# Weighted sums of the first heads moved ahead of a query tile, and four of sixteen picks of seven heads summed on another engine

## The chip, the cores and the metric

One core of a Trainium2 chip runs the whole program. The metric is the device time of one execution in microseconds (us). The engines are TensorE (PE), VectorE (DVE), ScalarE (ACT), GpSimd (POOL) and SyncE (SP), and 16 DMA engines move data.

## What is computed

Two transformer blocks on 512 tokens of width 1024. All that the change touches is the last stage of the second one, a mixture of 16384 experts with one row each, of which every token takes 16 in each of 8 heads. Shortened:

```python
def peer_ffn(x, w_q, k1, k2, down, up):
    # per block of 128 tokens
    q = x @ w_q                                  # 8 heads x 256
    s1, s2 = q1 @ k1, q2 @ k2                    # 128 scores each
    t1, t2 = top16(s1), top16(s2)
    w, idx = top16(all pairs t1 + t2)            # 16 of 256
    g = softmax(w)
    h = gelu(x . down[idx])                      # one dot per pick
    return sum(g * h * up[idx])                  # over 8 heads x 16 picks
```

The result is added to the residual, normalised and stored.

## The kernel before

The tokens lie in 4 tiles of 128, one token on each partition. A *head* in the code is one of 32 pairs of a token tile and a head of the expert stage (`N_HEADS`); head i belongs to tile i // 8. Each head has 16 *picks*, so there are 512, numbered n = 16 i + s. For a pick, an indirect DMA, issued by POOL in the function `gather`, fetches one row of `peer_rows` for each of the 128 tokens: 8 KB, `down` in its first half and `up` in its second, 1 MB in all. It lands in one of the buffers of `pair`. There are 7 of these at first; 6 more come in at picks 75, 76, 83, 107, 108 and 120 (`MORE_PAIRS`).

What happens to pick s of head i, in order:

- `dot(i, s)` on DVE (line 2534) multiplies the `down` half by the tokens and sums it over the row.
- `expert_weights(i, b)` on ACT takes the GELU of two such sums, b = s // 2; `weights(i, b)` on DVE (line 2541) multiplies them by the softmax; ACT then writes two diagonal matrices with the weights on the diagonal (`diag`, 12 buffers). `head_weights(i, first, stop)` is a run of such pairs. Within it, ahead of pair 5, stands `softmax_exp(i + 2)`.
- `weighted(i, first, stop)` on PE (line 1120) multiplies each diagonal by the `up` half in two matmuls and adds the product up in PSUM. Its end (`up_used`) is what the next gather into that buffer waits for.

DVE also runs the search of the top 16 for a later head, in steps between the dots (`best_keys` to `expert_numbers`, lines 2427 to 2499). In head 0 (`first_head`) these are the steps of heads 1 and 2.

At the same time the query projection is still being computed for all heads: 16 tiles, `query(t)` on PE, 24 matmuls each, and `peer_scores(h)` behind each pair. The weights of a tile come by a DMA of SP into a ring of few slots, and are split into two parts: ACT writes the high part (`query_high`, called high(t) here), and POOL subtracts it for the low part (`query_low`, low(t) here, line 2699). The load of tile t from 6 on waits for the end of `query(t - 2)`. POOL works its list in order: gathers 0 to 4, low(5), gathers 5 and 6, low(6), gathers 7 to 10, low(7), gathers 11 to 14, low(8), gathers 15 to 18, low(9), gathers 19 to 22, and so on to low(15). So gather 11 stands behind low(7), which stands behind high(7) on ACT.

No scheduler is at work: every engine runs its instructions in the order in which they are written, and waits on semaphores. ACT's list starts as

```python
peer_scores(1); query(4); query(5); query_high(6)
head_weights(0, 0, 2); peer_scores(2); softmax_exp(1)
head_weights(0, 2, 6); query_high(7); query(6)
head_weights(0, 6, 10); query_high(8); query(7)
head_weights(0, 10, 14); query_high(9); peer_scores(3)
```

where `query` and `peer_scores` on ACT copy PE's result out of PSUM. ACT's table of functions has to be loaded anew (`ACT_TABLE_LOAD`) between GELU and Exp.

## Time and profile before

| | |
|---|---|
| median of 3 runs | 3074.2 us (3073.37 to 3075.46) |
| the profiled execution's own time | 3077.88 us |
| its span in the profile | 3076.1 us |
| PE busy | 2693.7 us (88%) |
| DVE busy | 1747.6 us (57%) |
| POOL busy | 1157.1 us (38%) |
| ACT busy | 881.3 us (29%) |
| gathers (queue q0) | 73728 packets, 536.90 MB |

The page cuts the span into 40 slices of 77 us. The row of GB/s rises from 22 in slice 22 to 150, 339, 409, 411 and then stands at 427 to the last slice but one, while PE falls from nine tenths to seven. The stage of the gathers is the stretch from 1750 us to the end. A row of a stretch (windows) gives the busy time of each engine in it, the granted clock of PE as a share of 2.4 GHz, the busy share of the DMA engines and what they moved.

### The profile page before, as it was taken

How to read it: one execution, taken by the hardware profiler on the slowest of the kernel's cores; microseconds unless marked ns; L12 is line 12 of the kernel's file. 1: busy time of each engine (PE TensorE's matmuls, PEld its weight loads, DVE VectorE, ACT ScalarE, POOL GpSimd, SP SyncE). 2: the span in 40 equal slices, each digit the busy share in tenths (PEclk: the TensorE clock that was granted, in tenths of full speed). 3: DMA queues.
4: the chain of work that ended last, by engine and by line, in shares of the span. 5: the costliest groups of instructions: out<-in, count | busy, mean ns of one | idle time of the engine just before them, and what ended most of it. 6: DMA issues, size and time to landing. Idle time of an engine off the chain costs nothing.

```text
span 3076.1 us, 29817 instructions
## 1 busy us (share of the span) xinstructions
PE 2693.7 (88%) x10970; PEld 1857.5 (60%) x10970; DVE 1747.6 (57%) x3667; ACT 881.3 (29%) x1677; POOL 1157.1 (38%) x763
## 2 busy tenths in 40 slices
PE   6999999989989999899978899988777777777776
PEld 4999899977668888788837755543323233322222
DVE  5666762032747604322175477767777777777665
ACT  3111132134542224222142333333222222222221
POOL 1222233223934444423110355545444444444441
PEclk8999999989999999999988999999999999999999
DMA  6455431212025523212200489999999999999996
GB/s 244 158 182 176 162 127 57 62 62 76 22 69 169 173 96 94 91 62 69 71 0 22 150 339 409 411 427 427 427 427 427 427 427 427 427 427 426 427 427 288
DMA packets 125231, 722.07 MB, mean 235 GB/s; under 512 B 14864, under 2 KB 16144, under 8 KB 58288
## 3 DMA queue, kind: packets, MB, share of 16 engines
q0 software_dynamic: 73728, 536.90, 41.7%
q1 hardware_dynamic: 35920, 127.74, 12.1%
q10 hardware_dynamic: 15456, 55.80, 5.6%
q8 instruction: 72, 1.18, 0.1%
q14 instruction: 55, 0.45, 0.0%
HBM read 718.29 MB, written 2.10 MB: 234 GB/s over the span
## 4 chain that ended last, share of the span: by engine, by line
PE 58%; DMA 27%; DVE 9%; ACT 3%; issue 2%; POOL 1%; SPq 0%; ACTq 0%; DVEq 0%; POOLq 0%
PE acc L619 14%; PE acc L620 14%; PE acc L621 14%; DMA wring<-in_peer_rows,squares 9%; DMA hid<-in_peer_rows,squares 8%; PE sums L1120 5%; DMA arena<-in_peer_rows,squares 4%; DMA resid<-in_peer_rows,squares 3%; PE acc L1120 3%; PE sums L552 1%; DMA modw<-in_peer_rows,squares 1%; DVE hid L2534 1%; DVE squares L1924 1%; ACT hid L1179 1%; PE acc L843 1%
## 5 line engine op out<-in xcount | busy, mean ns | idle before, releaser
L2699 POOL TENSOR_TENSOR wring_parts<-wring,wring_parts 128x1024 fp32r<-128x1024 f32 (+1 forms) x215 | 524.2, 2449 | 1180.8 <-ACT wring_parts L1179 1180.6
L619 PE MATMUL acc<-hid_parts,wring_parts 128*128 128x384 f32 (+1 forms) x2152 | 796.2, 370 | 48.6 <-DVE hid_parts L1871 19.6
L621 PE MATMUL acc<-hid_parts,wring_parts 128*128 128x384 f32 (+1 forms) x2152 | 777.2, 361 | 0.0
L620 PE MATMUL acc<-hid_parts,wring_parts 128*128 128x384 f32 (+1 forms) x1656 | 598.6, 361 | 0.0
L619 PEld LDWEIGHTS acc<-hid_parts,wring_parts 128*128 128x128 f32 x2152 | 407.9, 190 | 116.5 <-issue 50.2
L621 PEld LDWEIGHTS acc<-hid_parts,wring_parts 128*128 128x128 f32 x2152 | 407.5, 189 | 38.5
L1179 ACT ACTIVATE wring_parts<-wring 128x1024 fp32r<-128x1024 f32 (+1 forms) x215 | 223.1, 1040 | 514.0 <-DMA wring<-in_w_ffn_out 196.7
L620 PEld LDWEIGHTS acc<-hid_parts,wring_parts 128*128 128x128 f32 x1656 | 314.9, 190 | 32.9 <-issue 5.5
L2711 POOL DMA_INDIRECT arena<-in_peer_rows,squares x180 | 200.5, 1114 | 244.8 <-PE acc L1120 153.4
L1179 ACT ACTIVATE hid<-hid 128x2 f32<-128x2 f32 (+2 forms) x293 | 67.1, 229 | 764.6 <-DVE arena L2534 237.6
L2711 POOL DMA_INDIRECT wring<-in_peer_rows,squares x158 | 176.7, 1118 | 199.3 <-PE acc L1120 144.2
L620 PE MATMUL acc<-arena_parts,wring_parts 128*128 128x384 f32 (+1 forms) x656 | 236.4, 360 | 0.0
L2711 POOL DMA_INDIRECT hid<-in_peer_rows,squares x109 | 116.1, 1065 | 152.6 <-PE acc L1120 122.5
L1946 DVE TENSOR_TENSOR arena<-squares,acc 128x384 f32<-128x384 f32 (+1 forms) x66 | 39.5, 599 | 219.7 <-ACT squares L1179 219.7
L2534 DVE SCALAR_TENSOR_TENSOR arena<-arena,resid 128x1024 f32<-128x1024 f32 x101 | 127.2, 1260 | 47.0 <-DMA arena<-in_peer_rows,squares 46.4
L2534 DVE SCALAR_TENSOR_TENSOR arena<-arena 128x1024 f32<-128x1024 f32 x79 | 96.9, 1227 | 61.1 <-DMA arena<-in_peer_rows,squares 60.8
L620 PEld LDWEIGHTS acc<-arena_parts,wring_parts 128*128 128x128 f32 x656 | 123.2, 188 | 13.4 <-issue 0.7
L1974 DVE SCALAR_TENSOR_TENSOR resid<-acc,halfg,resid 128x384 f32<-128x384 f32 (+3 forms) x32 | 16.2, 547 | 199.0 <-PE acc L621 199.0
L1179 ACT ACTIVATE squares<-acc 128x384 f32<-128x384 f32 (+1 forms) x66 | 34.8, 527 | 321.8 <-PE acc L621 269.4
L2534 DVE SCALAR_TENSOR_TENSOR wring<-wring,arena 128x1024 f32<-128x1024 f32 x78 | 95.6, 1226 | 52.7 <-DMA wring<-in_peer_rows,squares 52.3
L2534 DVE SCALAR_TENSOR_TENSOR wring<-wring,resid 128x1024 f32<-128x1024 f32 x80 | 101.0, 1263 | 42.2 <-DMA wring<-in_peer_rows,squares 41.7
L1120 PE MATMUL acc<-arena,tmp 128*128 128x512 f32 x184 | 88.6, 617 | 24.9 <-ACT tmp L1179 24.9
(422 smaller groups left out, 4284.1 us busy)
## 6 DMA issues: line engine op xcount, KB each, us to landing
wring<-in_w_ffn_in SPq DMA_DIRECT2D x88, 512.0 KB, 4.7
modw<-in_w_ada ACTq DMA_DIRECT2D x56, 512.0 KB, 3.6
modw<-in_w_mod ACTq DMA_DIRECT2D x48, 512.0 KB, 3.8
wring<-in_w_ffn_out SPq DMA_DIRECT2D x32, 512.0 KB, 3.5
wring<-in_w_in SPq DMA_DIRECT2D x28, 512.0 KB, 3.4
wring<-in_w_mix_in SPq DMA_DIRECT2D x18, 512.0 KB, 3.4
wring<-in_peer_w_q SPq DMA_DIRECT2D x16, 512.0 KB, 5.7
wring<-in_w_ffn_out SPq DMA_DIRECT2D x16, 384.0 KB, 3.1
```

The lines of the kernel that those rows point to most:

```text
L552: return nc.tensor.matmul(o, w, x, start=(k == 0), stop=(k == last))
L619: nc.tensor.matmul(o, wh, high, start=first, stop=False)
L620: nc.tensor.matmul(o, wh, low, start=False, stop=False)
L621: return nc.tensor.matmul(o, wl, high, start=False, stop=last)
L843: mm = nc.tensor.matmul(acc[:, 2 * side + hf, 0:HALF], qT[rows, both, t * P:(t + 1) * P], kdup[rows, both // 2, hf * HALF:(hf + 1) * HALF] ...
L1120: mm = nc.tensor.matmul(o[:, hf, :], diag[n % N_DIAG], pair[PAIR_OF[n]][:, D + hf * 512:D + (hf + 1) * 512], start=(at == 0), stop=(at == ...
L1179: return nc.scalar.activation(o, i, func, **kw)
L1924: ins = V.scalar_tensor_tensor(o, Mw[:, x % 2, k, :], col, o, ALU.mult, ALU.add)
L1946: free(V.tensor_tensor(arena[:, (f * sides + hf) * width:(f * sides + hf + 1) * width], sg[:, (base + u) % 2, 0:width], acc[:, 2 * ((base ...
L2534: V.scalar_tensor_tensor(rows, rows, 1.0, xb[i // PEER_H], ALU.mult, ALU.mult, accum_out=p_dot[:, s:s + 1]).then_inc(dots_done, 1)
L2699: nc.gpsimd.tensor_tensor(Wlor[:, p, 0:blocks, 0:cols], Wlo[:, p, 0:blocks, 0:cols], Whir[:, p, 0:blocks, 0:cols], ALU.subtract).then_inc( ...
L2711: nc.gpsimd.indirect_dma_start(pair[PAIR_OF[n]], None, a["peer_rows"], bass.IndirectOffsetOnAxis(ap=idx_all[:, n:n + 1], axis=0)).then_inc ...
```

## The change

First, the order on PE and ACT in head 0. The weighted sum of picks 0 and 1 now stands ahead of the sixth query tile, `query(5)`; picks 2 to 5 stand ahead of `peer_scores(2)`, picks 6 and 7 ahead of `query(6)`, picks 8 to 11 ahead of `query(7)`, 12 and 13 ahead of `peer_scores(3)`. ACT's list follows: the first pair of weights ahead of the copies of `query(4)` and `query(5)` and of high(6), `softmax_exp(1)` behind six picks instead of two, high(7) behind eight instead of six, high(8) behind twelve instead of ten.

Second, in heads 0 to 6 the picks s = 1, 5, 9 and 13 (28 in all, `BY_VECTOR`) are taken off PE. ACT writes no diagonal for them. DVE multiplies the `up` half by the weight and adds it to `vector_sum`, 1024 columns of constants no longer in use; `vector_pick(i, s)` stands right behind `dot(i, s + 1)`. The gather into the buffer of such a pick waits for DVE (`vector_used`). `finish(0)` adds `vector_sum` to the sum in PSUM. POOL's list and SP's are as before.

```diff
 FIRST_PAIRS = 7
 MORE_PAIRS = {75: 7, 76: 8, 83: 9, 107: 10, 108: 11, 120: 12}
+BY_VECTOR = [i * PEER_K + s for i in range(7) for s in (1, 5, 9, 13)]
+BY_TENSOR = [_n for _n in range(N_PICKS) if _n not in BY_VECTOR]
+
+
+def tensor_picks(n):
+
+    return n - sum(m < n for m in BY_VECTOR)
...
                 for n in range(i * PEER_K + first, i * PEER_K + stop):
-                    at = n % SLOTS
-                    pe.wait_ge(diag_ready, n + 1)
+                    if n in BY_VECTOR:
+                        continue
+                    at, d = n % SLOTS, tensor_picks(n)
+                    pe.wait_ge(diag_ready, d + 1)
...
             query(4)
+            pe.wait_ge(tile_read, 1)
+            weighted(0, 0, 2)
             query(5)
+            weighted(0, 2, 6)
             peer_scores(2)
-            pe.wait_ge(tile_read, 1)
-            weighted(0, 0, 4)
+            weighted(0, 6, 8)
             query(6)
-            weighted(0, 4, 8)
+            weighted(0, 8, 12)
             query(7)
-            weighted(0, 8, 12)
+            weighted(0, 12, 14)
             peer_scores(3)
-            weighted(0, 12, 16)
+            weighted(0, 14, 16)
...
             peer_scores(1)
+            head_weights(0, 0, 2)
             query(4)
+            query_high(6)
             query(5)
-            query_high(6)
-            head_weights(0, 0, 2)
+            head_weights(0, 2, 6)
             peer_scores(2)
             softmax_exp(1)
-            head_weights(0, 2, 6)
+            head_weights(0, 6, 8)
             query_high(7)
             query(6)
-            head_weights(0, 6, 10)
+            head_weights(0, 8, 12)
             query_high(8)
             query(7)
-            head_weights(0, 10, 14)
+            head_weights(0, 12, 14)
             query_high(9)
...
+            def vector_pick(i, s):
+
+                n = i * PEER_K + s
+                if n in BY_VECTOR:
+                    k = BY_VECTOR.index(n)
+                    up, weight = pair[PAIR_OF[n]][:, D:2 * D], p_w[:, s:s + 1]
+                    dve.wait_ge(weights_ready, i * (PEER_K // BATCH) + s // BATCH + 1)
+                    if k == 0:
+                        V.tensor_scalar(vector_sum, up, weight, None, ALU.mult).then_inc(vector_used, 1)
+                    else:
+                        dve.wait_ge(vector_used, k)
+                        V.scalar_tensor_tensor(vector_sum, up, weight, vector_sum, ALU.mult, ALU.add).then_inc(vector_used, 1)
...
-                if PAIR_FREE[n]:
-                    pool.wait_ge(up_used, PAIR_FREE[n])
+                before = PAIR_FREE[n]
+                if before is not None and before in BY_VECTOR:
+                    pool.wait_ge(vector_used, BY_VECTOR.index(before) + 1)
+                elif before is not None:
+                    pool.wait_ge(up_used, tensor_picks(before) + 1)
```

How the instructions stand on ACT from the copy of `peer_scores(1)` to the first two diagonals, before. Line 1179 is the helper that every ACTIVATE goes through; `resid<-acc` copies a query tile, `wring_parts<-wring` is a high part, `hid<-hid 128x2` the GELU of a pair, `squares`, `modrows` and `tmp<-cst,hid` are diagonals:

```order
L1179 ACTIVATE arena<-acc 128x4x256 [waits acc_ready]
L1179 ACTIVATE resid<-acc 128x512 [waits acc_ready] x2
L1179 ACTIVATE wring_parts<-wring 128x1024 [waits w_loaded0]
L1179 ACT_TABLE_LOAD
L1179 ACTIVATE hid<-hid 128x2 [waits dots_done]
L1179 ACTIVATE squares<-cst,hid 128x128 [waits weights_ready]
L1179 ACTIVATE squares<-cst,hid 128x128
```

And in the changed kernel, where the helper is line 1194:

```order
L1194 ACTIVATE arena<-acc 128x4x256 [waits acc_ready]
L1194 ACT_TABLE_LOAD
L1194 ACTIVATE hid<-hid 128x2 [waits dots_done]
L1194 ACTIVATE squares<-cst,hid 128x128 [waits weights_ready]
L1194 ACTIVATE resid<-acc 128x512 [waits acc_ready]
L1194 ACTIVATE wring_parts<-wring 128x1024 [waits w_loaded0]
L1194 ACTIVATE resid<-acc 128x512 [waits acc_ready]
```

The GELU of picks 0 and 1 and the one diagonal left of them moved ahead of both query copies and of high(6).

The second place, ACT from `peer_scores(2)` on, before. `hid<-hid 128x16` is the exponential of a softmax; the high part is high(7):

```order
L1179 ACTIVATE arena<-acc 128x4x256 [waits acc_ready]
L1179 ACT_TABLE_LOAD
L1179 ACTIVATE hid<-hid 128x16 [waits top_ready]
L1179 ACT_TABLE_LOAD
L1179 ACTIVATE hid<-hid 128x2 [waits dots_done]
L1179 ACTIVATE squares<-cst,hid 128x128 [waits weights_ready]
L1179 ACTIVATE squares<-cst,hid 128x128
L1179 ACTIVATE hid<-hid 128x2 [waits dots_done]
L1179 ACTIVATE modrows<-cst,hid 128x128 [waits weights_ready]
L1179 ACTIVATE modrows<-cst,hid 128x128
L1179 ACTIVATE wring_parts<-wring 128x1024 [waits w_loaded1]
```

And now, the weights of picks 6 and 7 being the pair between the second table load and high(7):

```order
L1194 ACTIVATE arena<-acc 128x4x256 [waits acc_ready]
L1194 ACT_TABLE_LOAD
L1194 ACTIVATE hid<-hid 128x16 [waits top_ready]
L1194 ACT_TABLE_LOAD
L1194 ACTIVATE hid<-hid 128x2 [waits dots_done]
L1194 ACTIVATE modrows<-cst,hid 128x128 [waits weights_ready]
L1194 ACTIVATE modrows<-cst,hid 128x128
L1194 ACTIVATE wring_parts<-wring 128x1024 [waits w_loaded1]
L1194 ACTIVATE resid<-acc 128x512 [waits acc_ready]
```

Picks 2 to 5 left this place for one ahead of `peer_scores(2)`; high(7) still follows the exponential, and now stands behind picks 6 and 7 as well.

## Rows read from the trace of the kernel before

**Rows 1.** The page: the span, and the queue of the gathers.

```profile
span 3076.1 us, 29817 instructions
...
q0 software_dynamic: 73728, 536.90, 41.7%
```

**Rows 2.** The chain that ended last: start, us, what.

```profile
3061.49 1.24 DVE hid L2534 x2
```

**Rows 3.** Stretches of the stage: busy (instructions) of PE, PEld, DVE, ACT, POOL; clock, DMA, GB/s.

```profile
1775.00:1800.00 25.00, 25.00 (x75) 14.35 (x74) 22.09 (x61) 8.64 (x19) 14.56 (x10) 0.92 0.80 289
1800.00:1850.00 50.00, 47.73 (x160) 27.36 (x159) 34.86 (x91) 19.66 (x42) 27.42 (x21) 1.00 0.98 379
1850.00:1900.00 50.00, 44.75 (x137) 24.64 (x136) 37.97 (x88) 14.81 (x36) 29.21 (x21) 0.98 1.00 411
1900.00:1950.00 50.00, 48.07 (x145) 25.96 (x144) 35.05 (x85) 15.94 (x37) 27.74 (x21) 0.98 1.00 410
1950.00:2000.00 50.00, 46.99 (x164) 27.47 (x163) 35.65 (x115) 14.03 (x36) 21.57 (x20) 0.97 1.00 411
...
2100.00:2300.00 200.00, 156.02 (x337) 62.28 (x336) 149.34 (x404) 59.24 (x154) 92.05 (x82) 0.97 1.01 427
```

**Rows 4.** Stretches of 5 us, the same columns.

```profile
1770.00:1775.00 5.00, 1.38 (x2) 0.84 (x3) 2.81 (x7) 4.00 (x7) 2.34 (x1) 0.70 0.52 216
1775.00:1780.00 5.00, 5.00 (x8) 1.84 (x7) 3.51 (x11) 3.56 (x7) 0.96 (x1) 0.62 0.17 26
```

**Rows 5.** POOL in order of time: start us, us, then what ended the idle time.

```profile
1777.65 0.96 POOL L2711 DMA_INDIRECT hid<-in_peer_rows,squares  x1 [4.62 <-PE sums L1120]
...
1785.31 2.40 POOL L2699 TENSOR_TENSOR wring_parts<-wring,wring_parts 128x1024 fp32r<-128x1024 f32 x1
1790.89 0.96 POOL L2711 DMA_INDIRECT arena<-in_peer_rows,squares  x1 [3.18 <-PE sums L1120]
...
1803.22 0.96 POOL L2711 DMA_INDIRECT arena<-in_peer_rows,squares  x1 [3.69 <-PE sums L1120]
...
1813.90 1.84 POOL L2711 DMA_INDIRECT wring<-in_peer_rows,squares  x1 [0.16 <-issue]
```

**Rows 6.** ACT in order of time: high(6), table load, diagonals, exponential, copy.

```profile
1769.55 1.06 ACT L1179 ACTIVATE wring_parts<-wring 128x1024 fp32r<-128x1024 f32 x1 [1.80 <-DMA wring<-in_peer_w_q]
1770.63 1.28 ACT L1179 ACT_TABLE_LOAD   x1
...
1773.08 0.69 ACT L1179 ACTIVATE squares<-cst,hid 128x128 f32<-128x128 f32 x2 [0.95 <-DVE hid L2541]
...
1777.10 0.31 ACT L1179 ACTIVATE hid<-hid 128x16 f32<-128x16 f32 x1 [1.12 <-DVE hid L2463]
...
1788.93 0.60 ACT L1179 ACTIVATE resid<-acc 128x512 f32<-128x512 f32 x1 [3.91 <-PE acc L621]
```

**Rows 7.** DMA issues by line: count, KB each, median us from issue to landing.

```profile
wring<-in_peer_w_q SPq DMA_DIRECT2D x16, 512.0 KB, 5.7
```

**Rows 8.** DVE in order of time: a step of head 1's search, two dots.

```profile
1763.45 0.41 DVE L2447 TENSOR_TENSOR hid<-hid 128x256 f32<-128x256 f32 x1
...
1827.35 1.23 DVE L2534 SCALAR_TENSOR_TENSOR hid<-hid,resid 128x1024 f32<-128x1024 f32 x1 [0.80 <-DMA hid<-in_peer_rows,squares]
...
1848.86 4.00 DVE L2534 SCALAR_TENSOR_TENSOR hid<-hid,resid 128x1024 f32<-128x1024 f32 x1 [0.52 <-DMA hid<-in_peer_rows,squares]
```

**Rows 9.** PE in order of time: `query(4)`'s first and last matmul, `peer_scores(2)`, picks.

```profile
1755.97 0.48 PE L619 MATMUL acc<-hid_parts,wring_parts 128*128 128x512 f32 x1
...
1761.29 0.39 PE L621 MATMUL acc<-hid_parts,wring_parts 128*128 128x512 f32 x1
...
1767.86 2.02 PE L1086 MATMUL acc<-modw,resid 128*128 128x128 f32 x16 [0.73 <-issue]
1773.62 3.75 PE L1120 MATMUL sums<-hid,squares 128*128 128x512 f32 x4 [3.74 <-ACT squares L1179]
...
1811.10 3.60 PE L1120 MATMUL sums<-wring,squares 128*128 128x512 f32 x8
```

More of the change, by code:

```diff
@@ L130 @@
     PAIR_OF.append(_slot)
-    PAIR_FREE.append(_last.get(_slot, -1) + 1)
+    PAIR_FREE.append(_last.get(_slot))
     PAIR_USE.append(PAIR_OF.count(_slot))
@@ L511, in build @@
         dots_done, gelu_ready, weights_ready = sem("dots_done"), sem("gelu_ready"), sem("weights_ready")
-        diag_ready, up_used = sem("diag_ready"), sem("up_used")
+        diag_ready, up_used, vector_used = sem("diag_ready"), sem("up_used"), sem("vector_used")
+        at = CONST["dup0"][0]
+        vector_sum = cst[:, at:at + D]
         ssq_ready, fstd_ready, fin_ready = sem("ssq_ready"), sem("fstd_ready"), sem("fin_ready")
@@ L1116, in weighted @@
                 for n in range(i * PEER_K + first, i * PEER_K + stop):
-                    at = n % SLOTS
-                    pe.wait_ge(diag_ready, n + 1)
+                    if n in BY_VECTOR:
+                        continue
+                    at, d = n % SLOTS, tensor_picks(n)
+                    pe.wait_ge(diag_ready, d + 1)
                     for hf in range(2):
-                        mm = nc.tensor.matmul(o[:, hf, :], diag[n % N_DIAG], pair[PAIR_OF[n]][:, D + hf * 512:D + (hf + 1) * 512],
+                        mm = nc.tensor.matmul(o[:, hf, :], diag[d % N_DIAG], pair[PAIR_OF[n]][:, D + hf * 512:D + (hf + 1) * 512],
                                               start=(at == 0), stop=(at == SLOTS - 1))
@@ L1734, in expert_weights @@
                 for n in range(first, first + BATCH):
-                    if n >= N_DIAG:
-                        act.wait_ge(up_used, n - N_DIAG + 1)
-                    run(diag[n % N_DIAG], ident, ACT.Copy, scale=p_w[:, n % PEER_K:n % PEER_K + 1]).then_inc(diag_ready, 1)
+                    if n in BY_VECTOR:
+                        continue
+                    d = tensor_picks(n)
+                    if d >= N_DIAG:
+                        act.wait_ge(up_used, d - N_DIAG + 1)
+                    run(diag[d % N_DIAG], ident, ACT.Copy, scale=p_w[:, n % PEER_K:n % PEER_K + 1]).then_inc(diag_ready, 1)
             def final_std(t):
@@ L2542, in weights @@
                                 ALU.mult).then_inc(weights_ready, 1)
+            def vector_pick(i, s):
+                n = i * PEER_K + s
+                if n in BY_VECTOR:
+                    k = BY_VECTOR.index(n)
[6 more added lines that the diff above has]
+                        V.scalar_tensor_tensor(vector_sum, up, weight, vector_sum, ALU.mult, ALU.add).then_inc(vector_used, 1)
             def finish(t):
@@ L2550, in finish @@
                     emptied(dve, UNIT["rows"] + w)
-                dve.wait_ge(up_used, (t + 1) * SLOTS)
-                V.tensor_tensor(sum_, total[:, :, :].rearrange("p a n -> p (a n)"), g2row,
-                                ALU.mult).then_inc(tile_read, 1)
+                dve.wait_ge(up_used, tensor_picks((t + 1) * SLOTS))
+                products = total[:, :, :].rearrange("p a n -> p (a n)")
+                if t == 0:
+                    dve.wait_ge(vector_used, len(BY_VECTOR))
+                    link(V.tensor_tensor(vector_sum, vector_sum, products, ALU.add))
+                    products = vector_sum
+                V.tensor_tensor(sum_, products, g2row, ALU.mult).then_inc(tile_read, 1)
                 dve.wait_ge(tile_read, CREDIT + t + 1)
@@ L2572, in head @@
                 dot(i, 2)
+                vector_pick(i, 1)
                 if more:
@@ L2586, in head @@
                 dot(i, 6)
+                vector_pick(i, 5)
                 if more:
@@ L2600, in head @@
                 dot(i, 10)
+                vector_pick(i, 9)
                 if more:
@@ L2614, in head @@
                 dot(i, 14)
+                vector_pick(i, 13)
                 if more:
@@ L2629, in first_head @@
                 dot(0, 2)
+                vector_pick(0, 1)
                 best_pairs(1)
@@ L2643, in first_head @@
                 dot(0, 6)
+                vector_pick(0, 5)
                 key_numbers(1)
@@ L2656, in first_head @@
                 dot(0, 10)
+                vector_pick(0, 9)
                 best_pairs(2)
@@ L2670, in first_head @@
                 dot(0, 14)
+                vector_pick(0, 13)
                 key_numbers(2)
```

## The prediction

> **What bounds the kernel now.** I read the page first. The span is 3076.1 us, and 536.90 MB of it go through the gathers' queue [rows 1], 512 picks of 1.049 MB. Then the chain that ended last: its final link out of the DMA is the dot at 3061.49 [rows 2], and 14.6 us of sums and normalising follow. Then the stretches [rows 3]: from 2100 on the DMA engines are full (share 1.01) at 427 GB/s, with PE at 78% and DVE at 75%. A gather costs 1.049 MB / 427 GB/s = 2.46 us there, and nothing on PE or DVE makes that shorter. So the change can only move the end by what it does to the DMA engines' idle and slow time before 2000.
>
> How much is that? Against 427 GB/s, the five stretches from 1775 to 2000 [rows 3] lack 25 x 138/427 = 8.1 us, 50 x 48/427 = 5.6, 1.9, 2.0 and 1.9: 19.5 us. One hole is plain: shares of 0.52 and 0.17 between 1770 and 1780 [rows 4] are 2.4 + 4.2 = 6.6 us idle. It begins when gathers 0 to 6 have landed; gather 7 is issued only at 1777.65, after waiting for PE [rows 5]. The DMA engines take it up some 1.6 us after the issue (share 0.17 of the 5 us up to 1780).
>
> PE is no strict bound there. It is busy 89 to 100% [rows 3], and four picks fewer per head would free about 1.75 us each (3.60 us for two picks, which overlap a little [rows 9]): 28 picks, 49 us. DVE takes 28 x 1.23 = 34 us more [rows 8]; it is busy 166 of 225 us [rows 3], 74%, and goes to some 83%. Both lie beside a full DMA, and I cost both at nothing; if DVE were late, the buffers would come free later, and that is the third rival.
>
> **Part one, the earlier first sums.** Step by step, with durations of before.
>
> - Gathers 7 to 10. DVE ends head 1's `candidates` at 1763.9 [rows 8], so weights(0, 0) is at 1764, the diagonal just behind, and pick 0 starts on PE at about 1764.6 instead of 1773.62 [rows 9]. PE had ended `query(4)` at 1761.7 [rows 9] and idled 3 us. Pick 0 takes 3.55 us at the lower clock as before (3.75 with overlap, granted 0.70 and 0.62 [rows 4, 9], mostly the 1.2 GHz level). POOL is not free, though: low(6) needs high(6), which waits for its load and runs at 1769.55 to 1770.6 [rows 6] in both orders; low(6) then takes 2.4 us [rows 5]. Gather 7 goes out at 1773.2, 4.4 us earlier. Gather 8 (a buffer that DVE frees) follows at 1775.3. `query(5)` on PE, 5.7 us [rows 9], now ends at 1773.8, its copy 0.6 later [rows 6], and only then comes the GELU of picks 2 and 3: they are used at 1777.1 and 1778.8, gathers 9 and 10 go out right behind. The first hole shrinks from 6.6 to 2.3 us (1772.6 to 1774.9).
>
> - Gather 11. Pick 4 is done at 1781.6, `peer_scores(2)` 2.0 us later [rows 9], its copy at 1784.6. Then table load 1.28, the exponential and its sum 0.5, table load 1.28 [rows 6]: 1787.7. Before, all this stood behind two picks and ahead of the GELU of picks 2 and 3. Now it delays picks 6 and 7, whose diagonals end at 1788.9, and behind them high(7), 1.06 [rows 6], and low(7), 2.4: 1792.4. Gather 11 goes out at 1792.5, against 1790.89 [rows 5], although its buffer was free at 1781.6. The four gathers 7 to 10 with one weight load of 0.524 MB (1.2 us) keep the DMA for 11.1 us, to 1786.0; it then idles until 1794.2: 8.2 us.
>
> - Gather 15. PE was idle for 5 us, so picks 6 and 7 take 3.55 + 1.8, to 1794.0, and `query(6)` ends at 1799.5; the load for tile 8 waits for it. Its copy 1800.3, GELU and weights of picks 8 and 9 at 1800.8. Then DVE has two dots, a vector pick and search steps of head 2 (3 x 1.23 [rows 8] and about 2 us, an estimate) before the second exponential can run: 1806.5. Exponential, table load, GELU, weights, two diagonals (0.7 [rows 6]): 1809.5; high(8), low(8): 1813.1. Gather 15 goes out at 1813.2 against 1803.22 [rows 5]: 10 us late. DMA idle from 1805.3 to 1814.9: 9.6 us.
>
> - Gather 19. Picks 10 and 11 restart PE again, 1809.3 to 1814.6; `query(7)` to 1820.0; the load for tile 9 is issued only then and takes some 5.7 us [rows 7]; high(9) and low(9) to 1829.0. Gather 19 goes out at 1829.2 against 1813.90 [rows 5]: 15 us late. DMA idle 1826.0 to 1830.9: 4.9 us.
>
> So the holes are 2.3 + 8.2 + 9.6 + 4.9 = 25 us by gather 19. To see the net I compare landings: the dot of pick 21 waited for its DMA and started at 1827.35 before [rows 8]; now gathers 19 to 21 land at 1830.9 + 3 x 2.46 + 1.5 = 1839.8. **The stream is 12.5 us behind.**
>
> **Part two, the picks on DVE.** After that PE needs per head 4 picks less, 33 us against 16 x 2.46 + 2 x 1.2 = 42 us of DMA, and POOL finds free buffers. From 1827 to 2000 before lacks 23/50 of 5.6, 1.9, 2.0 and 1.9, which is 8.4 us. That is the most which can come back. Six weight loads fall there, and the stretches with them stay at 410 or 411 GB/s even where the share reads 1.00 [rows 3], so part of it belongs to the loads. Bounds 0 and 8.4; I take 5, since slots handed back late are the larger part of the first piece only. The extra addition in `finish(0)` is one DVE instruction of 1.2 us at about 2190, under a full DMA: nothing.
>
> **Sum:** +12.5 - 5 = +7.5 us. The profiled execution took 3077.88 us on a span of 3076.1; its span would become 3083.6. The median of the runs is 3.7 us under the profiled execution, and the difference carries over: 3074.2 + 7.5 = **3081.7 us**.
>
> **The clock.** Three of the steps above restart PE after 3, 5 and 6 us idle. After 3.74 us idle before, the granted clock was 0.62 to 0.70 and pick 0 took twice its time [rows 4, 9]. If PE came back at 2.4 GHz, each step is 1.75 us earlier, 5.3 in all.
>
> **The rivals.**
>
> A, close to no change. PE restarts at full clock and most of the 8.4 us comes back: 12.5 - 5.3 - 5 = +2.2, or -1.2 with all of 8.4. Time 3073 to 3080. For it: the idle before pick 0 is shorter than any row here with a slow restart. Against: the other two are longer.
>
> B, faster. The sequence works as a pipeline: low(7) does not decide when gather 11 goes out, the buffer does. That holds if high(7) can run before the DMA has worked off gathers 7 to 10, at 1786. Then only the first hole's gain of 4.3 us and up to 8.4 us of later slack count: 3061.5 to 3068. For it: the buffers of picks 4 and 5 are free by 1782. Against: high(7) stands behind the exponential on ACT by the order of the list, and that needs `peer_scores(2)`, which now stands behind pick 4.
>
> C, much slower. DVE and POOL hold each other up: the dot at 1848.86 took 4.00 us instead of 1.23 [rows 8] while POOL worked. With 28 more two-input instructions on DVE, three such collisions in the chain of gathers 11, 15 and 19 and none of the 5 us regained give 12.5 + 3 x 2.8 = +21: 3095.
>
> The Trainium skill ("SBUF — State Buffer", "SBUF: two separate sides") says that DVE and GpSimd share a port pair as an exclusive lock, which a DVE instruction with two SBUF inputs takes against a GpSimd one that reads SBUF. The dot of 4.00 us agrees. By that rule rival C's collisions would come whenever low(t) and a vector pick meet.
>
> **How the numbers follow.** The forecast (+5 to +13) gets 0.44, A 0.30, B 0.16, C 0.10. A range from 3067 to 3090 holds the forecast, A and the upper end of B, and leaves C and the rest of B out. A measurement tells 0.2% (6 us) from no change. Slower by more than that holds C and most of the forecast: 0.50. Same, A and the lower end of the forecast: 0.35. Faster: 0.15.
>
> **What would show it.** In the profile after: gather 7 issued near 1773; gather 11 not before low(7), at about 1792; gathers 15 and 19 at 1813 and 1829; DMA shares far below 1 near 1790, 1810 and 1828, and none after 1850; ACT's idle time before high(7), (8), (9) ended by PE and DVE, not by the loads for 7 and 8. If gather 11 goes out before 1786, the forecast falls and B stands. If the holes are there and the end is still early, the later slack was larger than 8.4 us and my reading of the stretches is wrong.

## The result, and the profile after

| | before | after |
|---|---|---|
| median | 3074.2 us (3071.91 to 3083.08, 5 runs) | 3099.73 us (3097.04 to 3105.35, 5 runs) |
| ratio | | 1.0082, 95% interval 1.0062 to 1.0102 |
| the profiled execution | 3077.88 us, span 3076.1 | 3104.81 us, span 3103.0 |

The change makes the kernel 25.5 us slower. The forecast was 7.5 us slower, 3081.7 us, with a range that ended at 3090: the sign is right, the size is not, and the time lies outside the range.

The page of the changed kernel: the span, and the same queue as in [rows 1].

```profile
span 3103.0 us, 29619 instructions
...
q0 software_dynamic: 73728, 536.90, 41.4%
```

The same stretches as [rows 3], two more between them (columns: busy time of PE, PEld, DVE, ACT, POOL, the granted clock, the DMA share, GB/s):

```profile
1775.00:1800.00 25.00, 18.21 (x58) 10.64 (x59) 15.57 (x43) 7.82 (x15) 12.53 (x9) 0.86 0.65 250
1800.00:1850.00 50.00, 35.37 (x106) 20.28 (x105) 30.68 (x76) 12.74 (x26) 17.98 (x13) 0.86 0.69 261
1850.00:1900.00 50.00, 42.22 (x136) 24.70 (x135) 39.85 (x83) 13.51 (x32) 27.48 (x20) 0.93 0.96 390
1900.00:1950.00 50.00, 39.51 (x120) 21.43 (x120) 42.54 (x96) 13.75 (x32) 27.67 (x20) 0.97 1.00 411
1950.00:2000.00 50.00, 42.20 (x139) 24.06 (x138) 39.83 (x95) 16.87 (x38) 29.36 (x25) 0.97 0.96 396
2000.00:2050.00 50.00, 35.53 (x95) 15.94 (x95) 42.31 (x113) 12.29 (x31) 26.70 (x21) 0.93 1.01 427
2050.00:2100.00 50.00, 36.32 (x135) 19.65 (x133) 28.80 (x77) 12.75 (x26) 17.07 (x16) 0.90 1.01 420
2100.00:2300.00 200.00, 157.93 (x371) 66.72 (x371) 150.13 (x417) 58.10 (x152) 95.12 (x85) 0.97 0.99 414
```

Against 427 GB/s they lack 10.4, 19.4, 4.3, 1.9, 3.6, 0, 0.8 and 6.1 us (each is the length times the missing share of 427, as the prediction reckoned), 46.5 us together. Before it was 19.5 us. The difference, 27.0 us, is the difference of the spans, 26.9. So the ledger of lost DMA time holds all of the loss. It has two large entries, 29.8 against 13.7 us up to 1850 and 6.9 against 0 after 2050, and a small one of 4.0 between them: from 1850 to 2000 the changed kernel lacks 9.8 us, the kernel before 5.8.

The holes in stretches of 5 us, to be read beside [rows 4]:

```profile
1785.00:1790.00 5.00, 0.74 (x1) 0.50 (x2) 1.79 (x6) 4.71 (x9) 0.00 (x0) 0.70 0.66 277
1790.00:1795.00 5.00, 5.00 (x9) 1.98 (x7) 4.93 (x19) 0.45 (x1) 4.10 (x2) 0.62 0.00 0
...
1805.00:1810.00 5.00, 0.54 (x1) 0.50 (x2) 3.52 (x9) 2.88 (x7) 0.00 (x0) 0.75 0.62 256
1810.00:1815.00 5.00, 5.00 (x9) 1.93 (x7) 4.93 (x10) 0.64 (x1) 4.12 (x2) 0.57 0.01 3
1825.00:1830.00 5.00, 1.20 (x11) 1.01 (x10) 1.58 (x5) 1.35 (x2) 0.21 (x1) 1.00 0.58 242
1830.00:1835.00 5.00, 2.37 (x3) 1.18 (x4) 4.25 (x9) 1.55 (x5) 4.55 (x3) 0.63 0.07 11
...
2105.00:2110.00 5.00, 3.07 (x14) 1.70 (x13) 2.48 (x11) 1.81 (x4) 2.37 (x2) 1.00 0.22 43
```

In the three holes up to 1835 PE is nearly idle just ahead (0.74, 0.54 and 1.20 of 5 us) and then restarts at a granted clock of 0.57 to 0.63, the 1.2 GHz level in the main.

POOL in order of time, beside [rows 5]: gather 7, low(7), gather 11, low(8), gather 15, low(9), gather 19, gather 21, and the two gathers around the late hole.

```profile
1774.98 0.95 POOL L2758 DMA_INDIRECT hid<-in_peer_rows,squares  x1
...
1790.53 2.34 POOL L2743 TENSOR_TENSOR wring_parts<-wring,wring_parts 128x1024 fp32r<-128x1024 f32 x1 [8.55 <-ACT wring_parts L1194]
1793.02 1.76 POOL L2758 DMA_INDIRECT arena<-in_peer_rows,squares  x1 [0.15 <-issue]
...
1810.72 3.10 POOL L2743 TENSOR_TENSOR wring_parts<-wring,wring_parts 128x1024 fp32r<-128x1024 f32 x1 [12.09 <-ACT wring_parts L1194]
1813.97 1.23 POOL L2758 DMA_INDIRECT arena<-in_peer_rows,squares  x1 [0.15 <-issue]
...
1829.79 2.34 POOL L2743 TENSOR_TENSOR wring_parts<-wring,wring_parts 128x1024 fp32r<-128x1024 f32 x1 [10.87 <-ACT wring_parts L1194]
1832.28 1.84 POOL L2758 DMA_INDIRECT wring<-in_peer_rows,squares  x1
...
1836.69 1.19 POOL L2758 DMA_INDIRECT hid<-in_peer_rows,squares  x1 [1.07 <-PE sums L1133]
...
2095.79 0.94 POOL L2758 DMA_INDIRECT hid<-in_peer_rows,squares  x1 [1.27 <-PE sums L1133]
2107.32 0.94 POOL L2758 DMA_INDIRECT resid<-in_peer_rows,squares  x1 [10.59 <-PE acc L1113]
```

POOL waits for ACT's high part ahead of each low part, as predicted, and the gathers behind it go out in one bunch. The late hole is a wait of 10.59 us of gather 120 for `residual_tokens(3)` on PE (line 1113).

ACT between `peer_scores(2)` and high(7), beside [rows 6]: the copy, table load, exponential, table load, GELU, diagonals, high part.

```profile
1784.33 1.02 ACT L1194 ACTIVATE arena<-acc 128x1024 f32<-128x1024 f32 x1 [3.86 <-PE acc L1097]
1785.37 1.28 ACT L1194 ACT_TABLE_LOAD   x1
1786.66 0.31 ACT L1194 ACTIVATE hid<-hid 128x16 f32<-128x16 f32 x1
...
1787.08 1.28 ACT L1194 ACT_TABLE_LOAD   x1
1788.38 0.20 ACT L1194 ACTIVATE hid<-hid 128x2 f32<-128x2 f32 x1
1788.81 0.69 ACT L1194 ACTIVATE modrows<-cst,hid 128x128 f32<-128x128 f32 x2 [0.23 <-DVE hid L2560]
1789.41 1.04 ACT L1194 ACTIVATE wring_parts<-wring 128x1024 fp32r<-128x1024 f32 x1
```

And PE around it, beside [rows 9]: `peer_scores(2)` ends at 1784.3, and picks 6 and 7 come after 4.97 us of idle time. Picks 10 and 11 and picks 14 and 15 wait likewise.

```profile
1782.34 1.95 PE L1097 MATMUL acc<-modw,resid 128*128 128x128 f32 x16
1789.26 3.78 PE L1133 MATMUL sums<-wring,modrows 128*128 128x512 f32 x4 [4.97 <-ACT modrows L1194]
...
1809.46 3.78 PE L1133 MATMUL sums<-arena,modrows 128*128 128x512 f32 x4 [5.38 <-ACT modrows L1194]
...
1832.63 3.78 PE L1133 MATMUL sums<-hid,tmp 128*128 128x512 f32 x4 [6.43 <-ACT tmp L1194]
```

Each of the three ends with diagonals of ACT, and together (16.8 us) they are most of the 20.0 us that PE is idle from 25 to 100 us after gather 0. What kept ACT differs. Ahead of the first it is the two table loads and the exponential, with no transfer in the chain. Ahead of the second the exponential had waited 3.52 us for DVE's search (1806.86). Ahead of the third high(9) had waited 6.27 us for its load (1828.65).

DVE, beside [rows 8]: the dot of pick 21, and a vector pick (`cst<-`) that met a low part on POOL.

```profile
1844.87 1.23 DVE L2553 SCALAR_TENSOR_TENSOR hid<-hid,resid 128x1024 f32<-128x1024 f32 x1 [1.08 <-DMA hid<-in_peer_rows,squares]
...
1851.53 3.40 DVE L2574 SCALAR_TENSOR_TENSOR cst<-hid,cst 128x1024 f32<-128x1024 f32 x1
```

The chain that ended last is links of the gathers' DMA down to one of 25.83 us at 3062.56, as before [rows 2]: after the holes the stream is full again, and nothing is made up.

### The profile page after: what moved, and what is told of

Same layout as the page of the kernel before. It is cut to its first block, busy times and chain, and to the rows that moved or that the text cites. A ratio compares the mean times of both kernels' runs of the same rounds, so it can differ in the third digit from the quotient of the medians.

```text
span 3103.0 us, 29619 instructions
## 1 busy us (share of the span) xinstructions
PE 2671.2 (86%) x10858; PEld 1844.1 (59%) x10858; DVE 1782.4 (57%) x3696; ACT 872.9 (28%) x1649; POOL 1157.6 (37%) x763
## 4 chain that ended last, share of the span: by engine, by line
PE 55%; DMA 28%; DVE 10%; ACT 3%; issue 3%; POOL 1%; SPq 0%; ACTq 0%; DVEq 0%; POOLq 0%
PE acc L630 14%; PE acc L631 13%; PE acc L632 13%; DMA wring<-in_peer_rows,squares 8%; DMA hid<-in_peer_rows,squares 8%; DMA arena<-in_peer_rows,squares 7%; PE sums L1133 4%; PE acc L1133 3%; DMA resid<-in_peer_rows,squares 2%; PE sums L563 1%; DMA modw<-in_peer_rows,squares 1%; DVE hid L2553 1%; DMA modw<-in_w_mod 1%; DVE wring L2553 1%; ACT hid L1194 1%
## 5 line engine op out<-in xcount | busy, mean ns | idle before, releaser
L2758 POOL DMA_INDIRECT wring<-in_peer_rows,squares x158 | 169.0, 1070 | 214.3 <-PE acc L1133 152.7
L1993 DVE SCALAR_TENSOR_TENSOR resid<-acc,halfg,resid 128x384 f32<-128x384 f32 (+3 forms) x32 | 16.1, 546 | 203.1 <-PE acc L632 203.0
L1133 PE MATMUL acc<-arena,modrows 128*128 128x512 f32 x184 | 88.1, 614 | 25.8 <-ACT modrows L1194 25.8
```

The lines of the kernel that those rows point to most:

```text
L1133: mm = nc.tensor.matmul(o[:, hf, :], diag[d % N_DIAG], pair[PAIR_OF[n]][:, D + hf * 512:D + (hf + 1) * 512], start=(at == 0), stop=(at == ...
L1993: ins = V.scalar_tensor_tensor(x1, acc[:, b + bank, at:at + hi_ - lo], hgate[:, ffn, j, kind:kind + 1], x1, ALU.mult, ALU.add)
L2758: nc.gpsimd.indirect_dma_start(pair[PAIR_OF[n]], None, a["peer_rows"], bass.IndirectOffsetOnAxis(ap=idx_all[:, n:n + 1], axis=0)).then_inc ...
```

## The experiments

Single profiles are compared by two measures. *The stage* is the time from gather 0's start to the end of the span. *Lost* is the DMA time that a stretch lacks against 427 GB/s. Gather 0's own start lies anywhere from 1743 to 1757 in the profiles here, so times of different profiles are compared from gather 0 on. "A to B" below means us after gather 0.

| kernel | ratio, 95% | stage | lost 0-25 | 25-100 | 100-250 | 250-400 |
|---|---|---|---|---|---|---|
| before | | 1326.0 | 4.7 | 13.7 | 5.6 | 0 |
| before, again | 1.0011 (0.9996 to 1.0025) | 1330.2 | 4.7 | 14.1 | 10.2 | 0.4 |
| after | 1.0082 (1.0062 to 1.0102) | 1351.5 | 5.7 | 28.8 | 9.8 | 6.7 |
| after, again | 1.0083 (1.0066 to 1.01) | 1352.3 | 5.9 | 28.6 | 9.5 | 6.3 |
| order_only | 1.0047 (1.003 to 1.0064) | 1350.8 | 5.9 | 29.3 | 13.3 | 1.4 |
| order, again | 1.0073 (1.0044 to 1.0102) | 1348.8 | 5.9 | 29.2 | 10.5 | 1.4 |
| vector_only | 1.0028 (1.0013 to 1.0043) | 1340.9 | 4.6 | 18.1 | 8.4 | 8.4 |

**1. The halves apart.** First the new lists of PE and ACT without a pick on DVE (the diff is against before and cut to PE's list), then the picks on DVE with the old lists.

```diff
             query(4)
+            pe.wait_ge(tile_read, 1)
+            weighted(0, 0, 2)
             query(5)
+            weighted(0, 2, 6)
             peer_scores(2)
-            pe.wait_ge(tile_read, 1)
-            weighted(0, 0, 4)
+            weighted(0, 6, 8)
             query(6)
-            weighted(0, 4, 8)
+            weighted(0, 8, 12)
...
```

> The new order of TensorE and ScalarE in head 0, with no pick on VectorE. Queue theory (low(7), low(8) and low(9) stand ahead of gathers on GpSimd and now come late because ScalarE writes the high parts later): the three DMA holes near 1790, 1810 and 1830 us are there as in the changed kernel, time 3084 to 3093 us, that is 10 to 18 us over the kernel before. Vector theory (the 28 picks make VectorE late and buffers come back late): no such holes, 3072 to 3078 us.

Measured: 3094.93 us (4 runs) beside 3079.24 of before on the same chip. The order carries all of the first entry of the ledger: 29.3 us lost from 25 to 100 against 13.7, where the changed kernel loses 28.8.

```diff
+BY_VECTOR = [i * PEER_K + s for i in range(7) for s in (1, 5, 9, 13)]
...
+                if n in BY_VECTOR:
+                    k = BY_VECTOR.index(n)
...
```

> The 28 picks on VectorE with the order of before in head 0. Queue theory: within 5 us of the kernel before, since GpSimd's low parts come as before. Vector theory: 3085 to 3100 us, with the DMA short of gathers in the stretches between 1850 and 2110 us while VectorE's dots do not wait for any transfer.

Measured: 3091.12 us (6 runs) beside 3079.24. Not free: 4.4 us more are lost from 25 to 100, and 8.4 us from 250 to 400, where before loses none. By the stage the picks cost 12.8 us against the mean of the two profiles of before (1328.1), by the ratio 8.6. Whether the halves add up can't be told to a few us: by the stages order (21.7) and picks (12.8) are more than the whole (23.8), by the ratios (14.5 to 22.5, and 8.6) about the whole. In the changed kernel the picks' early cost doesn't show beside the order's (28.8 us lost from 25 to 100, against 29.3 without them); their late one does (6.7 us against 1.4).

**2. The low parts ahead of the gathers.** POOL takes each of low(7), low(8) and low(9) four gathers later, so that gathers 11, 15 and 19 stand ahead of them.

```diff
-            gathers(7, 11)
+            gathers(7, 15)
             query_low(7)
-            gathers(11, 15)
-            query_low(8)
             gathers(15, 19)
-            query_low(9)
+            query_low(8)
             gathers(19, 23)
+            query_low(9)
```

In the changed kernel:

> The changed kernel with GpSimd's list altered alone: low(7), low(8) and low(9) each stand behind four gathers more (gathers 7 to 14, low(7), 15 to 18, low(8), 19 to 22, low(9)). Queue theory: gather 11 goes out at 1784 to 1787 us instead of 1793.0, gather 15 about 8 us earlier than 1814.0; 8 to 14 us of the loss come back, 3086 to 3092 us. If the holes come from TensorE and VectorE alone: gather 11 waits for its buffer and the time stays at 3097 to 3102 us.

Measured: 3094.92 us (5 runs), ratio 1.0046 (1.0031 to 1.0061), stage 1343.7; 21.6 us lost from 25 to 100 instead of 28.8. Some 8 us come back by the profile. The rest doesn't: gathers 15 and 19 now wait 5.5 us each for PE's sums, and the late hole stays (7.4 us lost from 250 to 400). In the kernel before:

> The kernel before with one edit on POOL: gathers 7 to 14 ahead of low(7), gathers 15 to 18 ahead of low(8), 19 to 22 ahead of low(9). Theory (a low part ahead of gathers on POOL holds the DMA back): in the old order gather 11 waited for PE's sums for 3.18 us behind low(7), so the buffer and not the low part decided it; little is to be gained: -3 to 0 us, and low(7) comes about 4 us later, which query(7) on PE may pay for. Rival (the low parts cost as much in the old order as in the new, where moving them gave some 8 us back): -6 to -10 us, about 3070.

Measured: 3086.03 us (12 runs) beside 3077.07 (17 runs), ratio 1.0027 (1.0011 to 1.0042). A miss of both: in the old order the late low parts cost about 8 us. They hold up the query tiles on PE, where `query(7)` now waits 3.85 us for low(7) (PE busy 66.5 us from 25 to 100, against 72.7), and 20.4 us are lost there. With the new order alone:

> The kernel before with the new order on PE and ACT, no picks on DVE, and the low parts 7, 8 and 9 four gathers later on POOL. Run on one chip with the changed kernel, since the runs so far came from different chips. Theory (the low parts ahead of gathers 11, 15 and 19 cost some 8 of the order's 15 us): about 7 us over before, ratio 1.0015 to 1.003. Rival (the buffers of picks 4 to 12 come free that late anyway, behind the query tiles on PE, and the low part is not what decides): ratio 1.004 to 1.005, as the order alone.

Measured: 3091.6 us (6 runs) beside 3075.38 (11 runs), ratio 1.0049 (1.0033 to 1.0065): by the ratio the rival's number. The profile lies between the two: stage 1341.8, some 8 us under the order alone (1350.8 and 1348.8) as the theory has it, but 13.7 over before where it has 7; 23.2 us are lost from 25 to 100, 6 less than with the order alone. PE's wait ahead of picks 14 and 15 is 1.83 us there, against 5.95 in the order alone. That the low parts cost the new order some 8 us thus rests on single profiles, here and in the changed kernel; the ratios (1.0049 here, 1.0047 and 1.0073 for the order alone) don't show it. The rows say why no more is to be had. PE, `peer_scores(2)` and picks 6 and 7:

```profile
1782.30 1.95 PE L1086 MATMUL acc<-modw,resid 128*128 128x128 f32 x16
1789.21 3.78 PE L1120 MATMUL sums<-wring,modrows 128*128 128x512 f32 x4 [4.97 <-ACT modrows L1181]
```

It is the same 4.97 us as after: moving the low parts doesn't touch it.

**3. One hole filled.** ACT writes high(7) ahead of `peer_scores(2)` and the exponential.

```diff
+            query_high(7)
             peer_scores(2)
             softmax_exp(1)
             head_weights(0, 6, 8)
-            query_high(7)
```

> The changed kernel with one instruction of ScalarE moved: high(7) ahead of the copy of peer_scores(2) and the exponential. Queue theory: low(7) ends near 1785 us, gathers 11 and 12 fill about 5 us of the hole of 8 us near 1790, the holes near 1810 and 1830 stay; 3093 to 3097 us. Vector theory: no change, 3097 to 3102 us.

Measured: 3107.27 us (4 runs), ratio 1.0087 (1.006 to 1.0113), stage 1357.1. POOL, gather 11, then low(8) and gather 15:

```profile
1781.39 1.85 POOL L2758 DMA_INDIRECT arena<-in_peer_rows,squares  x1
...
1807.34 3.10 POOL L2743 TENSOR_TENSOR wring_parts<-wring,wring_parts 128x1024 fp32r<-128x1024 f32 x1 [14.31 <-ACT wring_parts L1194]
1810.59 1.23 POOL L2758 DMA_INDIRECT arena<-in_peer_rows,squares  x1 [0.15 <-issue]
```

Gather 11 goes out 33.3 us after gather 0 instead of 41.5, and gather 15 at 62.5, where it was. A miss: the first hole moved into the second (29.0 us lost, against 28.8). My reading is that no single gather's wait sets the pace, but the chain on PE and ACT that every fourth gather hangs on.

**4. A query tile as cover.** PE computes `query(6)` ahead of picks 6 and 7.

```diff
             peer_scores(2)
-            weighted(0, 6, 8)
             query(6)
-            weighted(0, 8, 12)
+            weighted(0, 6, 12)
```

> The changed kernel with TensorE's list altered alone: query(6) stands ahead of picks 6 and 7, in the 5 us in which TensorE waits for the exponential's chain. If query(6) behind picks 6 and 7 carries the delay to gathers 15 and 19: gather 15 goes out 5 to 7 us sooner after gather 0 (56 to 57 us instead of 62.5), 5 to 9 us of the loss come back. If low(t)'s place in GpSimd's list alone matters: gather 15 no sooner, no gain.

Measured: 3099.92 us (6 runs), ratio 1.0074 (1.0048 to 1.0101), stage 1344.7, 23.7 us lost from 25 to 100. POOL, low(8) and gather 15, 55.8 us after gather 0 instead of 62.5:

```profile
1803.37 2.34 POOL L2742 TENSOR_TENSOR wring_parts<-wring,wring_parts 128x1024 fp32r<-128x1024 f32 x1 [6.11 <-ACT wring_parts L1193]
1805.85 1.76 POOL L2757 DMA_INDIRECT arena<-in_peer_rows,squares  x1
```

The profile is 6.8 us shorter by the stage, as much as the theory forecast; the median doesn't show it, and the interval takes in both.

**5. The first pair alone.** Before, with only picks 0 and 1 ahead of `query(5)`.

```diff
             query(4)
+            pe.wait_ge(tile_read, 1)
+            weighted(0, 0, 2)
             query(5)
             peer_scores(2)
-            weighted(0, 0, 4)
+            weighted(0, 2, 4)
```

> The kernel before with one part of the new order: the weights and the sum of picks 0 and 1 ahead of query(4)'s and query(5)'s copies and of query(5); from peer_scores(2) on everything stands as before (the exponential behind two picks, high(7) behind six, query(6) behind four). No pick on VectorE. Queue theory: gather 7 goes out 3 to 5 us earlier after gather 0 and nothing later is late, so 0 to 4 us faster than before, within noise. If the early first sums themselves do the harm (TensorE stopped for 3 us ahead of query(5)): 5 us or more slower than before.

Measured: 3085.08 us (10 runs), ratio 1.0017 (1.0 to 1.0035). The stage is 1337.6, 9.5 us over the mean of before. Gather 7 goes out 23.3 us after gather 0 instead of 27.6, and gather 11 at 47.1 instead of 40.8. PE, picks 2 and 3:

```profile
1776.70 6.67 PE L1120 MATMUL sums<-arena,squares 128*128 128x512 f32 x8 [4.97 <-ACT squares L1180]
```

Before, PE did picks 0 and 1 behind `peer_scores(2)`, while ACT went through table load, exponential and table load. With these picks moved ahead, nothing covers that chain, and PE stands idle for the same 4.97 us as in the changed kernel. The earlier first gathers are the one gain that my working was sure of; moving the pair brings them at this price, and the whole is worth nothing, and rather costs.

**What the eight profiles without a pick on DVE in head 0 or 1 say together.** From 25 to 100, PE's idle time (75 less its busy time) and the DMA's lost time:

| | PE idle | lost |
|---|---|---|
| before | 2.3 | 13.7 |
| vector_heads_2_to_4 (below) | 2.3 | 14.1 |
| before, again | 5.3 | 14.1 |
| first_pair_only | 8.0 | 18.3 |
| before_pool_late_low | 8.5 | 20.4 |
| order_late_low | 13.9 | 23.2 |
| order, again | 17.9 | 29.2 |
| order_only | 18.1 | 29.3 |

Four of the rows they come from: before,

```profile
1775.10:1850.10 75.00, 72.73 (x233) 41.70 (x232) 56.95 (x151) 28.20 (x61) 42.09 (x31) 0.98 0.92 349
```

first_pair_only,

```profile
1768.71:1843.71 75.00, 67.04 (x218) 39.33 (x217) 50.08 (x136) 25.82 (x56) 35.48 (x26) 0.95 0.84 323
```

order_late_low,

```profile
1772.99:1847.99 75.00, 61.07 (x204) 36.38 (x203) 45.94 (x126) 23.51 (x51) 30.21 (x23) 0.95 0.79 295
```

and the order alone, again:

```profile
1781.59:1856.59 75.00, 57.11 (x179) 32.44 (x177) 42.11 (x117) 22.51 (x48) 28.41 (x21) 0.91 0.68 261
```

Over the whole of this table a us that PE stands idle goes with about one us that the DMA loses (15.8 more of the one and 15.6 of the other from its top to its end), though 3 us more of idle time in before's second profile cost 0.4. With four picks of each head taken off PE, part of its idle time is free: 10.7 idle and 18.1 lost in vector_only, 17.1 and 21.6 in after_pool_late_low, 18.0 and 23.7 in after_query6_ahead, 20.0 and 28.8 in after. I take it that PE and the loop through it (dot, GELU, weights, diagonal, sum, next gather, and the query tiles' high and low parts beside it) set the pace of these 75 us. That the two go together is measured; which of them leads isn't shown by it, except for the wait of 4.97 us, whose chain has no transfer in it.

**6. The picks on DVE.** Three variants of vector_only. The last extra buffer taken up at pick 128 instead of 120:

```diff
-MORE_PAIRS = {75: 7, 76: 8, 83: 9, 107: 10, 108: 11, 120: 12}
+MORE_PAIRS = {75: 7, 76: 8, 83: 9, 107: 10, 108: 11, 128: 12}
...
-                    if n == 120:
+                    if n == 128:
                         pool.wait_ge(acc_ready, UNIT["xtok"] + 4)
```

The second part moves POOL's wait for `residual_tokens(3)` along with the buffer.

> The kernel vector_only with the last of the added buffers coming in at pick 128 instead of 120, so that gather 120 no longer waits for the fourth residual transpose. If that wait, with few gathers in flight, makes the hole of some 6 us near 2090: the hole is gone and 4 to 6 us come back against vector_only. If VectorE is simply too slow there: the hole only moves.

Measured: 3083.07 us (10 runs), ratio 1.0017 (1.0003 to 1.0031), stage 1334.4. Picks on DVE in heads 0 to 3 only:

```diff
-BY_VECTOR = [i * PEER_K + s for i in range(7) for s in (1, 5, 9, 13)]
+BY_VECTOR = [i * PEER_K + s for i in range(4) for s in (1, 5, 9, 13)]
```

> The kernel vector_only with picks on VectorE in heads 0 to 3 alone (16 instead of 28). Vector theory (VectorE at 82% in heads 4 to 6 lets the store of gathers in flight run down until the wait at gather 120 empties it): no hole near 2090, 5 to 8 us come back against vector_only, within 2 to 6 us of the kernel before. If the cost lies in head 0: at most 2 us come back.

Measured: 3085.0 us (10 runs), ratio 1.0020 (1.0006 to 1.0034), stage 1331.4. The stretch from 2050 to 2100 in vector_only, with the slot later, and in four heads:

```profile
2050.00:2100.00 50.00, 32.22 (x87) 14.63 (x87) 34.03 (x95) 13.81 (x32) 21.56 (x18) 0.93 0.88 364
```

```profile
2050.00:2100.00 50.00, 33.88 (x91) 14.90 (x90) 35.75 (x98) 13.82 (x32) 21.67 (x20) 0.93 1.00 413
```

```profile
2050.00:2100.00 50.00, 42.05 (x127) 20.38 (x125) 32.27 (x96) 14.69 (x35) 25.46 (x23) 0.97 1.01 427
```

Either edit takes the late hole away. So it comes of two things that meet: gather 120's wait for `residual_tokens(3)`, and DVE's picks in heads 4 to 6, which hand the buffers back so late that few gathers are under way when POOL stops. The bytes agree: from gather 0 to the issue of gather 119 the DMA engines have moved 125.4 MB in before and 125.3 in four heads, but 128.0 in vector_only and 127.9 in the changed kernel (each added up from stretches), so of the same 120 gathers some 2.4 fewer are still under way, an estimate at 1.049 MB each. Before, POOL stops for the same reason (9.78 us, gather 120 at 2078.70), and no row of the DMA shows it.

The other loss of the picks is in heads 0 and 1: gather 11 goes out 44.4 us after gather 0 instead of 40.8. DVE in vector_only: the pick on DVE, a search step of 16 elements, and the dot behind them.

```profile
1785.23 1.28 DVE L2571 SCALAR_TENSOR_TENSOR cst<-wring,hid,cst 128x1024 f32<-128x1024 f32 x1
...
1787.14 3.03 DVE L2515 SCALAR_TENSOR_TENSOR squares<-hid 128x16 uint32<-128x16 f32 x1
1790.10 1.21 DVE L2550 SCALAR_TENSOR_TENSOR hid<-hid,resid 128x1024 f32<-128x1024 f32 x1
```

Then the picks where neither loss can arise, heads 2 to 4:

```diff
-BY_VECTOR = [i * PEER_K + s for i in range(7) for s in (1, 5, 9, 13)]
+BY_VECTOR = [i * PEER_K + s for i in range(2, 5) for s in (1, 5, 9, 13)]
```

> The old order, with VectorE summing four of sixteen picks in heads 2, 3 and 4 only. Theory (VectorE's work costs only where DMA and TensorE wait for it, in heads 0 and 1 and near 2090): gathers 11 to 39 as before within 1 us, ratio 0.999 to 1.001. Rival (every pick on VectorE hands its buffer back later): +2 to +4 us, 1.001 to 1.0015, lost in the stretch from 100 to 250 us after gather 0.

Measured: 3076.91 us (10 runs) beside 3079.3 (19 runs), ratio 0.9986 (0.9966 to 1.0006), stage 1328.0; gathers 11 to 39 within 0.5 us of before. There the picks cost nothing, and the interval doesn't show a gain either: from 100 to 250 us, where all of them lie, 8.1 us are lost, between the 5.6 and 10.2 of before's two profiles.

**7. Two repairs, one of them by half.** The changed kernel with the late low parts and the slot at pick 128. Unlike in vector_slot_later, POOL's line `if n == 120:` stays, and with it the wait for `residual_tokens(3)`.

```diff
-MORE_PAIRS = {75: 7, 76: 8, 83: 9, 107: 10, 108: 11, 120: 12}
+MORE_PAIRS = {75: 7, 76: 8, 83: 9, 107: 10, 108: 11, 128: 12}
...
-            gathers(7, 11)
+            gathers(7, 15)
```

> The changed kernel with two edits: the low parts 7, 8 and 9 four gathers later on POOL, and the last extra buffer taken up at pick 128 instead of 120. Theory (two separate losses: the low parts ahead of gathers 11, 15 and 19, and gather 120's wait for residual_tokens(3)): the two gains, some 8 to 11 us and 4 to 6 us, add up, 3082 to 3088 on a scale where before is 3079 and the changed kernel 3104; no hole in the DMA near 2090. Rival (the second hole only takes up slack that the first leaves): 3091 to 3095, as with the late low parts alone.

Measured: 3095.54 us (6 runs) beside 3077.07, ratio 1.0068 (1.0045 to 1.009), stage 1344.7. A miss of the theory, but no test of it: gather 120 no longer needs the new buffer, and still stands behind the wait that came with it. POOL stops for 10.60 us as in the changed kernel, at 2098.82:

```profile
2087.28 0.94 POOL L2758 DMA_INDIRECT hid<-in_peer_rows,squares  x1 [1.12 <-PE sums L1133]
2098.82 0.94 POOL L2758 DMA_INDIRECT hid<-in_peer_rows,squares  x1 [10.60 <-PE acc L1113]
```

From 250 to 400 us 6.3 us are lost, against 6.7 in the changed kernel and 1.8 in vector_slot_later, where gather 120 waits 3.75 us, for a sum on PE. So the late hole follows the wait and not the buffer. Whether the two gains add up with the wait moved as well wasn't run.

**8. The same kernels again.**

> The changed kernel once more, on the chip of the run beside it, to see how far its ratio moves from chip to chip: 1.006 to 1.010, with gather 11 behind low(7) near 42 us after gather 0, gather 15 near 62 and gather 19 near 81, and a DMA hole of some 7 us near 2100. If the stage from gather 0 to the end is not 1345 to 1355 us, the stage lengths of single profiles cannot be compared to 5 us.

> The kernel before once more. If gather 0's start moves from execution to execution: anywhere from 1743 to 1754, and 1326 us from there to the end within 2. If it were fixed for a kernel: 1750.1 within 1.

> The new order on PE and ACT alone once more. If the start moves from execution to execution: gather 0 anywhere from 1743 to 1754, 1351 us within 3 from there to the end, and over many executions a ratio nearer to 1.007. Rival (the order makes the start earlier): gather 0 at 1743 again and a ratio of 1.004 to 1.005.

Measured, in this order: ratio 1.0083, stage 1352.3, gathers 11, 15 and 19 at 41.5, 62.4 and 80.9, all as expected; gather 0 at 1744.71, stage 1330.2, so the start moves from execution to execution and the stage by some 4 us; gather 0 at 1756.59, stage 1348.8, 3100.95 us (4 runs) beside 3079.3, ratio 1.0073. The order doesn't make the start earlier, and its 1.0047 was the low end of its scatter: the order costs some 14 to 22 us, most of the 25.

No variant beats the kernel before by more than its interval.

## Why the prediction was wrong

**The bound from 2100 on** held: 427 GB/s and a share of 1.01 beyond the late hole, and the loss is DMA time lost earlier.

**Gathers 7 to 19** held. Gather 0 came 1.4 us later than before; less that, gather 7 went out at 1773.6 (predicted 1773.2), gather 11 at 1791.6 (1792.5), 15 at 1812.6 (1813.2), 19 at 1830.9 (1829.2). Low(7) waited for high(7), high(7) stood behind the exponential and picks 6 and 7, and PE restarted at the lower clock: rivals A and B fall by the same rows. High(9) waited 6.27 us for its load, as the working for gather 19 has it; that this also holds up `peer_scores(3)`'s copy and picks 14 and 15 behind it on ACT, and with them PE for 6.43 us, it doesn't say.

**The net by pick 21** was under by 3.6 us. Its dot came 77.25 us after gather 0 before and 93.37 after, 16.1 later against 12.5. I let gathers 19 to 21 land one behind the other from 1830.9; gather 21 went out only at 1836.69, 4.4 us after gather 19, and its dot started 8.2 us later.

**The 5 us regained** is the step that failed. From 100 to 250 us after gather 0 the changed kernel loses 9.8 and 9.5 us; before loses 5.6 in one profile and 10.2 in the other. I took 8.4 us of one profile for slack that a freer PE would hand back. Nothing of it came, and the second profile shows that this stretch moves by nearly as much from profile to profile. vector_heads_2_to_4 tests the step by itself: 12 picks taken off PE in this very stretch, 8.1 us lost and no gain beyond the interval. Nor did PE get 49 us freer: its busy time fell by 22.5 us, from 2693.7 to 2671.2. "PE is no strict bound" was a reading of one share per stretch: 72.7 of 75 us busy leaves 2.3 us, and the new order alone put some 15 us of idle time there and lost some 15 us of the DMA's.

**"Both cost at nothing"** failed too. DVE's share rose about as forecast from 1850 to 2000, from 72% to 81%: 39.85, 42.54 and 39.83 us of 50 against 37.97, 35.05 and 35.65 [rows 3]. Over the whole of 1775 to 2000, the prediction's stretch, it went from 74% to 75% only, being lower up to 1850. By vector_only the 28 picks cost some 9 to 13 us by themselves, in two places that a share doesn't show: 4 us in heads 0 and 1, where a dot is late for the next gather, and 6 to 8 us near 2100, through a wait of 10 us that stood in the trace of before all along. In the changed kernel the second is the one that shows, 6.7 us. I had read the waits of the stretch in which the change works, and none beyond 2000.

**Rival C** named a time near the result (3095) by a mechanism that is the smaller part. The collisions are there: 3.40 us for a vector pick that takes 1.28 elsewhere, and 3.03 us for a step of 16 elements. But a step of this kind took 2.63 us before as well, and ahead of each hole POOL waits for ACT's high part (8.55, 12.09 and 10.87 us), in the chain with PE. The Trainium skill ("SBUF — State Buffer", "SBUF: two separate sides") calls the shared port pair an exclusive lock for the whole instruction; the trace agrees, since the vector pick at 1851.53 is longer by 2.12 us beside a low part that POOL runs from 1851.22 on for 2.63 us. Which row starts first doesn't tell who is held: the dot at 1848.86 before took 4.00 us, although the low part's row starts 0.55 us behind it (1849.41).

The sum in the ledger's terms, against before's first profile: +1.0 up to 25 us, +15.1 from 25 to 100, +4.2 to 250 and +6.7 to 400, 27.0 us, where the stages differ by 25.5. The prediction had 12.5 for the first two, -5 for the third and 0 for the last. So it was 3.6 us short in the first two, 9.2 in the third and 6.7 in the last. Against the mean of before's two profiles the third is +1.9 in place of +4.2.

## What to carry to other kernels

In a stretch where an engine is busy 97% of the time, start from putting the idle time that a new order gives it in the sum one for one, even where the DMA isn't full either; it was less here where the engine had been given less to do. Ask of work that is moved what wait it had covered: picks 0 and 1 had covered the 4.97 us of the exponential's chain. A long wait of the engine that issues the transfers is harmless only while enough of them are under way: look through the whole stage for such waits before something is put at nothing because "the DMA is full there". And slack read from one execution is worth asking for twice, since the same program lost 5.6 us of DMA time in one and 10.2 in the other.
